# Router logits with the padded router weights stationary and the tokens moving, and the first hyena chunk among the first turnings

## What is computed

```python
u = rmsnorm(x, norm_mix)                       # here: squares, "turnings" (transposes), gains
q, k, v, hy, gates = split(u @ w_in)           # hyena part: short conv, FFT-like long conv
x = x + (g0 * attention + g1 * hyena) @ w_out
x = x + cross_attention(rmsnorm(x, norm_x), rmsnorm(mem, norm_mem))
h = rmsnorm(x, norm_ffn)
aff = softmax(h @ w_router)                    # 16 experts: the router logits
g, idx = top_k(aff.T, 2 * T // 16)             # each expert picks its tokens: 128 and 32
he = silu(xe @ w_gate) * (xe @ w_up)           # xe = h[idx]
x = x + scatter_add(he @ w_down * g)
out = rmsnorm(x, norm_final)
```

## Time and profile before

| | |
|---|---|
| median of 3 runs | 2747.7 us (2744.48 to 2748.73) |
| profiled execution | 2748.03 us, span 2746.2 us |
| busy: PE, DVE, ACT, POOL | 2640.7, 879.5, 417.7, 252.5 us |
| PE weight loads | 1779.1 us |
| mean granted TensorE clock | 0.982 |
| DMA | 315.78 MB, mean 115 GB/s |

### The profile page before, as it was taken

The page is one execution under the profiler, slowest core; times in us unless marked ns, Lnnn a source line. Parts: engine busy times, 40 slices in busy tenths (PEclk is TensorE's granted clock), DMA queues, the critical chain, the costliest instruction groups (busy, mean ns, idle before and its releaser), DMA issues.

```text
span 2746.2 us, 29716 instructions
## 1 busy us (share of the span) xinstructions
PE 2640.7 (96%) x12283; PEld 1779.1 (65%) x12283; DVE 879.5 (32%) x1526; ACT 417.7 (15%) x946; POOL 252.5 (9%) x270
## 2 busy tenths in 40 slices
PE   7999899999989999999999999977999999999997
PEld 4554454466567777764455476547788788778876
DVE  5566723166773121134300044362111111111112
ACT  3120000144451101102100022110000000000002
POOL 0120100000001001042000002000110010011001
PEclk9999999999999999999999999978999999999999
DMA  4110211000001010041011100136787778778776
GB/s 156 31 50 11 80 54 31 0 1 16 1 24 47 24 46 24 24 168 31 31 46 46 61 31 24 69 123 250 245 270 256 263 256 281 252 244 271 255 263 245
DMA packets 189938, 315.78 MB, mean 115 GB/s; under 512 B 6122, under 2 KB 69951, under 8 KB 189216
## 3 DMA queue, kind: packets, MB, share of 16 engines
q1 hardware_dynamic: 181952, 292.87, 30.8%
q0 software_dynamic: 7904, 21.76, 3.1%
HBM read 288.40 MB, written 26.21 MB: 115 GB/s over the span
## 4 chain that ended last, share of the span: by engine, by line
PE 89%; DVE 8%; ACT 1%; issue 1%; DMA 0%; POOL 0%; POOLq 0%; DVEq 0%; SPq 0%; ACTq 0%
PE banks L748 60%; PE banks L1030 9%; PE banks L929 5%; PE banks L1119 4%; PE banks L1244 3%; PE banks L949 2%; PE banks L1378 2%; DVE arena L1895 2%; PE banks L964 1%; PE banks L764 1%; PE banks L1348 1%; DVE arena L1752 1%; DVE arena L2279 0%; DVE arena L2282 0%; DVE arena L2395 0%
## 5 line engine op out<-in xcount | busy, mean ns | idle before, releaser
L748 PE MATMUL banks<-arena 128*128 128x160 f32 (+3 forms) x8070 | 1754.3, 379 | 24.8 <-ACT arena L1449 7.9
L748 PEld LDWEIGHTS banks<-arena 128*128 128x128 f32 x8070 | 1247.0, 191 | 538.7 <-issue 480.3
L1030 PE MATMUL banks<-arena 128*128 128x320 f32 x896 | 243.5, 433 | 2.6 <-DVE arena L2031 2.1
L634 POOL TENSOR_TENSOR arena<-arena 128x512 f32<-128x512 f32 (+1 forms) x72 | 109.5, 1533 | 1303.7 <-DMA arena<-in_w_br_hyena 759.0
L1030 PEld LDWEIGHTS banks<-arena 128*128 128x128 f32 x896 | 169.8, 190 | 72.4 <-issue 2.3
L2360 DVE TENSOR_TENSOR arena<-arena,banks 128x160 f32<-128x160 f32 x128 | 41.2, 321 | 521.6 <-ACT arena L1679 489.2
L1679 ACT ACTIVATE arena<-banks 128x160 f32<-128x160 f32 x120 | 36.4, 304 | 764.4 <-PE banks L748 764.4
L929 PE MATMUL banks<-arena 128*128 128x512 f32 (+1 forms) x384 | 144.7, 527 | 2.5 <-DVE arena L1935 2.5
L1119 PE MATMUL banks<-arena 128*128 128x512 f32 x280 | 122.6, 593 | 0.7 <-ACT arena L1589 0.7
L1995 DVE TENSOR_REDUCE att<-banks 128x1 f32<-128x1024 f32 (+1 forms) x80 | 81.4, 1059 | 129.8 <-PE banks L949 129.7
L929 PEld LDWEIGHTS banks<-arena 128*128 128x128 f32 x384 | 71.4, 193 | 56.6 <-issue 53.7
(11 more groups left out here) (237 smaller groups left out, 1591.6 us busy)
## 6 DMA issues: line engine op xcount, KB each, us to landing
arena<-in_w_exp_gate SPq DMA_DIRECT2D x32, 2048.0 KB, 8.0
arena<-in_w_exp_up SPq DMA_DIRECT2D x32, 2048.0 KB, 12.9
arena<-in_w_exp_down SPq DMA_DIRECT2D x32, 2048.0 KB, 17.8
arena<-in_w_in SPq DMA_DIRECT2D x36, 512.0 KB, 4.1
arena<-in_x_prompt SPq DMA_DIRECT2D x8, 1024.0 KB, 8.0
residual_rows<-arena SPq DMA_DIRECT2D x10, 512.0 KB, 2.6
normed_rows<-arena SPq DMA_DIRECT2D x10, 512.0 KB, 2.6
arena<-residual_rows SPq DMA_DIRECT2D x5, 1024.0 KB, 14.7
```

The costliest lines, as they stand in the source:

```text
L634: done.inc(pool.tensor_tensor(out, l, r, op))
L748: last = pe.matmul(out, l, r, start=(n == 0), stop=(n == len(pairs) - 1))
L1030: last = pe.matmul(PS[:, 3 * (g % 2) + bank, 0:GN], l[:, k, :], r[:, k, :], start=(k == 0 and which in (G1, G2, G5)), stop=(k == 3), skip_ ...
```

## The change

At the start, SP issues `hyena_load(0)` behind `x_load(1)`, ahead of the other three loads of x. PE turns tiles 0 to 3, waits for them to be complete in `UT`, and then puts the eight matmuls of `hyena_chunk(0, 0)` in twos ahead of the turnings of tiles 4 to 7. The chunk's place behind the filter products is left empty.

The router's weights get 32 columns a block (16 of them zero), and they are stationary now. `route(pair)` puts four of the eight blocks side by side in four column groups of the array, each with the 256 tokens of the pair moving, twice, so that bank 5 holds four partial sums of the logits, transposed. ACT copies them to `PARTS`. `logits(pair)` multiplies `PARTS`, 128 tokens at a time, with `fold` (four stacked identities of 16), which adds the four parts and turns them back. `fold` and the zero columns are made by DVE at the start. `rt_mm` now counts three a pair. For pairs 0 and 1 copy and fold come one round of the loop later; for pair 2 behind the loop; for pair 3 behind one more sample product; the sample's tiles 8 and 9 are both turned before their one `route`. Semaphores: the router's load counts on `rev_in`, and `lam_ready` is replaced by the step counter.

```diff
-            for i in range(1, NT // 2):
-                x_load(i)
+            x_load(1)
...
             hyena_load(0)
+            for i in range(2, NT // 2):
+                x_load(i)
...
-            for t in range(NT):
+            for t in range(4):
+                turn_rows(t)
+            wait("hy_in_0", 16)
+            wait("ut_ready", 8)
+            for m in range(4):
+                for k in (2 * m, 2 * m + 1):
+                    last = pe.matmul(PS[:, 0, :], HYW[0][:, k, :], UT[:, k, 0:512], start=(k == 0), stop=(k == KD - 1))
+                turn_rows(4 + m)
+            last.then_inc(sem["hy_mm"], 1)
+            for t in range(NTP, NT):
                 turn_rows(t)
...
-                    hyena_chunk(b, n, b % 3, 3 * (b % 2))
+                    if b or n:
+                        hyena_chunk(b, n, b % 3, 3 * (b % 2))
...
+            def route(pair):
+
+                for t in (2 * pair, 2 * pair + 1):
+                    wait("ut_ready", 2 * (N_FFN + t) + 2)
+                if pair:
+                    wait("rt_parts", pair)
+                cols = slice(2 * pair * P, 2 * (pair + 1) * P)
+                for m in range(KD // 4):
+                    for j in range(4):
+                        last = pe.matmul(PS[CS * j:CS * (j + 1), 5, 0:2 * P], rw[:, 4 * m + j, :], HT[:, 4 * m + j, cols],
+                                         start=(m == 0), stop=(m == KD // 4 - 1), tile_position=(0, CS * j))
+                last.then_inc(sem["rt_mm"], 1)
+
+            def logits(pair):
+
+                wait("rt_parts", pair + 1)
+                for n, t in enumerate((2 * pair, 2 * pair + 1)):
+                    s = logit_slot(t)
+                    product(PS[:, 4, s * NE:(s + 1) * NE], [(PARTS[:, tiles[n]], fold[:, :])]).then_inc(sem["rt_mm"], 1)
...
                 if i:
+                    if i >= 2:
+                        logits(i - 2)
                     turn_rows(N_FFN + 2 * i - 2)
...
                 if i:
-                    route(2 * i - 2)
-                    route(2 * i - 1)
+                    route(i - 1)
+            logits(XPAIRS - 2)
             sample_out(0, range(2))
...
-            route(NTP - 2)
-            route(NTP - 1)
-            sample_out(0, range(4, KD - 1))
+            route(XPAIRS - 1)
+            sample_out(0, range(4, 5))
+            logits(XPAIRS - 1)
+            sample_out(0, range(5, KD - 1))
...
                 turn_rows(N_FFN + t)
-                route(t)
+            route(XPAIRS)
+            logits(XPAIRS)
...
+            def parts_out(pair):
+
+                act.wait_ge(sem["rt_mm"], 3 * pair + 1)
+                act.copy(PARTS, PS[:, 5, 0:2 * P]).then_inc(sem["rt_parts"], 1)
...
                 out_kept(i, 0, G1)
+                if i >= 2:
+                    parts_out(i - 2)
                 if i:
                     out_normed(2 * i - 2)
...
+            parts_out(XPAIRS - 2)
             out_normed(NTP - 2)
             out_normed(NTP - 1)
+            parts_out(XPAIRS - 1)
...
+            dve.memset(rw[:, :, NE:CS], 0.0)
...
+            step.inc(dve.tensor_copy(fold[:, :], ident[:, 0:NE]))
+            for j in range(1, 4):
+                step.wait()
+                step.inc(dve.tensor_tensor(fold[:, :], fold[:, :], ident[:, CS * j:CS * j + NE], ALU.add))
```

More of the change, by code:

```diff
@@ L137 @@
 hy_in_0 hy_in_1 hy_in_2 hy_mm raw_ready pad_zero  conv_done z_ready z_tr zt_ready
-inv_mm  inv_used hz_ready wv_in v_mm v_ready lam_in  lam_sum lam_exp lam_ready
+inv_mm  inv_used hz_ready wv_in v_mm v_ready lam_in  lam_sum lam_exp
 wqk_in_0 wqk_in_1 rope_in qk_mm raw_qk q_roped k_roped
@@ L144 @@
 xs_mm  xmax_ready xexp_ready  xp_ready xp_tr pt_ready xo_mm ot_ready
-wx_in_0 wx_in_1 xo2_mm x2_ready acc_out acc_out_s hn_out_0 hn_out_1 wr_in rt_mm  rt_low rt_exp aff_ready aff_tr
+wx_in_0 wx_in_1 xo2_mm x2_ready acc_out acc_out_s hn_out_0 hn_out_1 rt_mm rt_parts rt_low rt_exp aff_ready aff_tr
  slots_ready slots_tr sorted_ready reversed idx_tr idx_ready eg0 eu0 eg1 eu1 ed0 ed1 col_ready gather_p gather_s xe_tr xet_ready
@@ L186, in encoder_kernel @@
         sub = small("sub", [P, 3, NT * HEADS])
-        rw = small("rw", [P, KD, NE])
+        rw = small("rw", [P, KD, CS])
+        fold = small("fold", [P, NE])
         idx_p, idx_q = small("idx_p", [P, NE], U32), small("idx_q", [P, NE], U32)
@@ L251, in encoder_kernel @@
         HT = OT
+        PARTS = at(191, 2 * P)
         LG, AFP, AFS = at(176, NT, NE), at(177, LP // 2)[0:2 * NE], at(179, LS)[0:NE]
@@ L460, in _ @@
             sp.dma_start(mirror[:, :], a["reverse"]).then_inc(sem["rev_in"], 16)
-            sp.dma_start(rw[:, :, :], blocked(a["w_router"][0], 0, NE)).then_inc(sem["wr_in"], 16)
+            sp.dma_start(rw[:, :, 0:NE], blocked(a["w_router"][0], 0, NE)).then_inc(sem["rev_in"], 16)
             for b in range(3, 2 * HG):
@@ L581, in _ @@
             sp.wait_ge(sem["xo2_mm"], 7 * XPAIRS + 4)
-            sp.wait_ge(sem["rt_mm"], NT)
+            sp.wait_ge(sem["rt_mm"], 3 * (XPAIRS + 1))
             sp.wait_ge(sem["gather_p"], 16)
@@ L1274, in _ @@
             cross_values(NT - 1)
-            def route(t):
-                wait("ut_ready", 2 * (N_FFN + t) + 2)
-                s = logit_slot(t)
-                product(PS[:, 4, s * NE:(s + 1) * NE], [(HT[:, k, tiles[t]], rw[:, k, :]) for k in range(KD)]).then_inc(sem["rt_mm"], 1)
-            wait("wr_in", 16)
+            def route(pair):
[14 more added lines that the diff above has]
+                    product(PS[:, 4, s * NE:(s + 1) * NE], [(PARTS[:, tiles[n]], fold[:, :])]).then_inc(sem["rt_mm"], 1)
+            wait("rev_in", 32)
+            wait("pad_zero", 7)
             for i in range(XPAIRS):
@@ L1328, in _ @@
             last.then_inc(sem["aff_tr"], 1)
-            wait("rev_in", 16)
+            wait("rev_in", 32)
             wait("sorted_ready", 1)
@@ L1670, in _ @@
             out_normed(NTP + 1)
+            parts_out(XPAIRS)
             act.wait_ge(sem["rt_low"], 2)
@@ L1954, in _ @@
             c.wait()
-            dve.tensor_scalar(lam[:, 0:1], lam[:, 0:1], -LAM_INIT, None, ALU.add).then_inc(sem["lam_ready"], 1)
+            c.inc(dve.tensor_scalar(lam[:, 0:1], lam[:, 0:1], -LAM_INIT, None, ALU.add))
             dve.wait_ge(sem["inv_mm"], 3 * HG)
-            dve.wait_ge(sem["lam_ready"], 1)
+            c.wait()
             dve.wait_ge(sem["rope_in"], 32)
@@ L2256, in affinities @@
             def affinities(turn_no, t0, n, bank, into):
-                dve.wait_ge(sem["rt_mm"], t0 + n)
+                dve.wait_ge(sem["rt_mm"], 3 * (t0 + n) // 2)
                 logits = PS[:, 4, t0 * NE:(t0 + n) * NE].rearrange("p (t e) -> p t e", e=NE)
```

## The result

The changed kernel takes 2725.4 us (median of 4 runs, 2724.25 to 2728.06), beside 2747.8 us for the kernel before (4 runs, 2744.48 to 2748.73): the ratio on record is 0.993, interval 0.9911 to 0.9947 (the two medians alone give 0.992). The kernel before was run again beside the later experiments; its 51 executions, these four among them, have a median of 2741.9 us and a mean of 2743.5: 26 of them lie between 2738.6 and 2741.9, 25 between 2744.5 and 2750.8, and none between. The first four all came from the upper group. The ten executions of the changed kernel, here and in e5, lie between 2724.2 and 2729.8 with a median of 2725.3 and a mean of 2726.0. So the change is worth 15 to 17.5 us: 15.1 by the medians side by side in e5, 16.5 by the medians of all executions, 17.5 by their means. The 22.4 us of the first comparison hold some luck.

A forecast was written before the change was run, and what follows sets the result against it. PE was taken as the bound, busy 96% of the span, with DVE the bound in the first turnings. Gains 3.1 + 10.5 + 2.4 + 0.2 = 16.2 us off 2748.03 gave 2731.8, stated as 2731.5 us; range 2725.5 to 2740.

The forecast's parts named there:

- start: First turnings with the hyena chunk's matmuls between them: net gain 3.1 us, from a loss of 3.9 to a gain of 5.4.
- loop: Router work in the loop over pairs: 6.4 us fewer records, 0.6 lost waiting, 4.7 clock given back; gain 10.5 us.
- last prompt pair: From tile 7 in place to the transposes, 8.5 us before: gain 0.5 to 4.2 by the clock, middle 2.4 taken.
- sample pair: Last router work, 3.53 us before, to take 3.3: gain 0.2 us, from a loss of 0.5 to a gain of 1.5.
- elsewhere: Rest of the kernel: no gain of its own; what follows the router starts from its results and moves along.
- The rival that the clock would not come back: Falls come from turnings and short waits, not the 16 columns; loop gives 5.8, last pair 0.5: 2738.1 us; chance 15%.
- The rule on drains: Switching tiling mode drains the engine: 0.38 us at each of ten switches, 3.8 us off the sum; not counted in it.
- The rival in which the groups do not overlap: Router's four column groups run one after another, 379 ns a record, 6.1 us for 16: about 2760 us; chance 3%.
- The prediction's chain of matmuls: Last prompt pair: packed matmuls 0.92, one matmul 0.87, fold 0.44, two matmuls 1.74: 4.0 us at full speed, 4.3 with waits.
- I take the value at full speed because the row at 20.63 has it: Start: the eight chunk matmuls priced at 0.87 us each, 7.0 us; all at half speed would cost 7.0 us more.
- The delay of x: Start: the hyena weights' earlier load makes tile 4's x late by nothing to 1.2 us; 0.4 taken.
- 2 us for the spread of the runs: Allowance for variation between runs, included in the range's lower end of 2725.5 us.

The follow-up runs named there:

- e5: The changed kernel run again with nothing edited: 2725.3 us over 6 executions, beside 2740.4 for the kernel before; ratio 0.9944.
- e6: Kernel before with the router's 16 moving columns repeated eight times, 128 in a matmul, so tokens are routed by other logits: 2734.0 us, ratio 0.9978.
- e7: Changed kernel without the packing: all eight router blocks one behind the other in the first column group, copy and fold kept: 2740.4 us, ratio 0.9992.
- e2: Kernel before with only the changed start, the router as before: 2743.0 us over 10 runs, ratio 0.9994.
- e9: The kernel before run once more with nothing edited, one run with its profile: 2740.5 us.
- e1: Changed kernel with the start as before, so the router's half alone: 2729.5 us, ratio 0.9944.
- e3: Changed kernel with two spare matmuls (512 and 128 columns) behind chunk (0, 1), meant to shift the later stream about 1 us: 2729.7 us, ratio 0.994.
- e10: The kernel before run a third time with nothing edited, one run with its profile: 2747.0 us.
- e4: Changed kernel with five tiles turned first, one chunk matmul ahead of each turning of tiles 5 to 9, three behind the last: 2730.8 us, ratio 0.9946.
- e12: The kernel of e8 run again, unedited, beside e11: 2723.2 us over 6 executions, ratio 0.9932 against the kernel before.
- e8: Kernel of e4 with the third pair's fold moved behind two sample matmuls: 2722.4 us over 6 executions, ratio 0.9933.
- e11: Kernel of e8 with spare 512-column matmuls into a free bank ahead of three of PE's waits (2, 2 and 4): 2719.8 us, ratio 0.9915.

## Why the prediction was right, and where not

The direction and the mechanism were right. The median, 2725.4, lies 6.1 us below the forecast of 2731.5 and 0.1 us below the range's lower end, 2725.5. Term by term, in the first two profiles:

| term | predicted | measured |
|---|---|---|
| start | 3.1 | 1.1 (96.57 - 95.50) |
| loop | 10.5 | 10.4 (below) |
| last prompt pair | 2.4 | 3.7 |
| sample pair | 0.2 | 0.0 |
| elsewhere | 0 | 8.8 - 0.2 |
| sum | 16.2 | 23.8 |

Without the 8.8 the measured terms add up to 15.0. That this is so near 16.2 is in part luck: the start was put 2.0 us too high and the last prompt pair 1.3 too low.

**Loop: right in the sum, and nearly so in its parts.** Until the first sample products of the loop are done it went from 1789.69 - 1712.91 = 76.78 to 1770.36 - 1703.00 = 67.36 us (1712.91 and 1703.00 are the first turnings), and the row behind from 8.05 to 7.03: 10.4 us. Packed 1.00 where 0.92 was said, fold 0.36 for 0.44, the wait 0.49 for 0.6, the 40 records 17.43 for 17.4. The split comes from e6, which has the old records and no fall: to the same product it takes 1776.51 - 1703.76 = 72.75 us, and the row behind 7.03. So 5.0 us are the clock (4.03 and 1.02) and 5.4 the records and the wait, where 4.7 and 5.8 were said. Two small misses cancel. The second pair's own records were slowed too, 3.79 us to the next start and not 3.49, which the prediction left out; and a packed row starts later behind its products, 3.53 us from start to start (1708.24 to 1711.77) where the old router's came after 3.43. PE's rows in the kernel before:

```profile
1718.15 3.60 PE L1244 MATMUL banks<-arena 128*128 128x512 f32 x8
...
1751.01 3.95 PE L748 MATMUL banks<-rw,arena 128*128 128x16 f32 x32
```

The rival that the clock would not come back is refuted by the rows at 1.00, and e6 shows what lowers the clock here: the narrow moving side, since the same records with 128 columns keep it.

**The rule on drains.** The prediction weighed the Trainium skill's rule (TensorEngine Tiling (Array Packing), Key Properties) that a switch of the tiling mode drains the engine. The 16 packed records took 1.00 us to the next start, where 16 x 57 ns is 0.92, and they start 0.10 us later behind the products: at most 0.18 us for a pair of switches, not twice 0.38. For five pairs that is 0.9 us (an estimate from the three of the loop), where the estimate by the rule took 3.8; the row was the nearer price, though its length, 3.66 us, does not show the start that comes later. The rival in which the groups do not overlap fell with it, and e7 shows its price: 3.58 us a pair, not 6.1. The prediction took the length of a record, 379 ns, for the time to the next one, which is 224 ns (3.58/16). It said that the gain would be used up at 213 ns a record, and e7, at 224, has none that the runs can tell.

**Last prompt pair: mis-sized, within its bounds.** From DVE's last write to the transposes it takes 1788.77 - 1784.26 = 4.5 us (it was 8.5), a gain of 4.0 where the middle of 0.5 and 4.2 was taken; 0.35 us go back into the turning's longer wait (1.43 for 1.08). PE ran at full clock behind two waits of 1.43 and 0.89 us, in every profile with the packed form. e6 has the old order there with dense columns, and its clock stays up as well (3.74 us for 32 records, against 4.94); but e7's falls there without the 16 columns, so the place has both clocks in it, as the prediction said. By e6, where the stretch from the turning of tile 6 to the transposes takes 11.04 us (14.37 before, 10.71 changed), 3.3 of the 3.7 us are the clock. The prediction's chain of matmuls leaves out DVE's softmax between the fold and the transposes: its last row ends at 1788.71, PE's last sample product at 1788.64, so fewer sample matmuls behind the fold would gain nothing more there.

**Start: mis-sized, by the clock.** The step that failed is "I take the value at full speed because the row at 20.63 has it". In the changed kernel's two profiles, and in e7's, the first hyena turning comes at 95.5 to 95.9; the first profile has four records at half speed (3.47 for 1.88, 1.6 us too long), and a fall at 38 us. With the same code e2 had neither and gained 4.1. So the term has a value between 1.1 and 4.1 by the clock that is granted at 21 and at 38 us. The old start varies as well: the first hyena turning comes between 96.13 and 97.55 in its five profiles, latest in e9, where the run behind the first product is 1.4 us longer (33.05 to 97.55). The delay of x, for which 0.4 was put in, cost nothing.

**Sample pair: right in kind.** Fewer records, but at half speed, and a wait of 0.48: 1833.74 - 1830.36 = 3.38 us for 3.53. From the affinities' transposes to the experts' first it takes 59.52 us, and 59.51 before.

**Elsewhere: the step that failed most.** "What follows moves along" and "2 us for the spread of the runs" took the shown execution for the kernel. It had falls of the clock behind waits that other executions don't have (by their times about half of them; profiles are there of three), and these are worth 8.8 us in the stretch up to the output products. Against e9, which has none of the three shown above, the changed kernel gains 2738.7 - 2722.4 = 16.3 us; against the 23 executions of before beside e5 15.1. The forecast of 16.2 fits these better than the one comparison that it was made for. What makes an execution fall into one group or the other stays open: the shift does not decide (e1 lay as before and held at 412 and 774; e3 missed its place). One thing goes with the fall at 412, though not always. Behind the wait of 2.9 us near 267 us the clock falls in some profiles (granted clock 0.51 to 0.64 in the next 3.4 us, against 1.00 in the others), at no cost, since PE waits for DVE there in any case. Of the thirteen profiles without fillers nine have that fall, and only one of these (e10) falls again at 412; the four without it (before, e2, e3, e4) all do. No run tells why.

## What to carry to other kernels

A matmul with few moving columns cost twice here: its own records took as long as their weight loads (PEld is busy 3.41 of 3.50 us in the first pair of the kernel before, and eight times the columns took 3.57 us for 3.49), and the clock it lowered slowed the wide matmuls behind it. So turning it round (narrow side stationary, in column groups, tokens moving) may pay more than its rows promise. Before a gain at one place is added up, compare several executions of the unchanged kernel stretch by stretch: here they fell into two groups whose means lie 6.7 us apart, and a stretch that nobody touched differed by 8 us between profiles. A fixed sum over rows is worth as much as the clock in those rows, so a term that starts behind a wait should carry both of its values into the range.

## What the runs showed of the hardware

- **An engine without idle time can lose its clock.** PE's rows show no wait through the 32 records with 16 moving columns, and yet 40 records behind them took 18.79 and 20.26 us (before, e2) instead of 17.4; with 128 columns they took 17.33 (e6). Behind the first pair it did not happen in any of the four profiles of the old router (17.41 us).
- **Falls behind the same wait are a matter of the execution.** Behind 3.65 us of waiting at 540 us the same 8 records took 3.78 us in one execution and 1.99 in another, with identical instructions ahead (before, e9). The Trainium skill (TensorE: Matmul & The Clock Gate, HAM oscillation) tells of waits that lower the clock in mid-kernel; the runs agree, and add that waits of 2.2 to 3.7 us (those of the rows beside e9 and e10) do so in some executions only.
- **Filling such waits with spare matmuls narrowed the runs**, from 8.8 and 12.1 us between the extremes (e12, e8; six executions each) to 1.9 (e11; five).
